# A two-layer diffusion step: the conditioning product moved out of the start and run in column groups, and attention scores issued in pairs

## The reference

```python
def _adaln(cvec, w, b):                      # w: (1024, 6144) for each layer
    m = (jax.nn.silu(cvec) @ w + b).reshape(-1, 1, 6 * D_MODEL)
    return jnp.split(m, 6, axis=-1)
for i in range(DEPTH):                       # DEPTH = 2
    mp = _adaln(c_ctx, mod_w[i], mod_b[i])   # context tokens
    ms = _adaln(c, mod_w[i], mod_b[i])       # latent tokens
    hp = _modulate(_rmsnorm(xp, norm1_g[i]), mp[0], mp[1])   # h * (1 + scale) + shift
    # layer 0: windowed attention (8 heads) and retention on h @ w_in, concatenated, @ w_out
    # layer 1: neighbourhood attention (16 heads) on h @ w_qkv, @ w_out
    xp = xp + mp[2] * op                     # gate
    hp = _modulate(_rmsnorm(xp, norm2_g[i]), mp[3], mp[4])
    # layer 0: dense SwiGLU; layer 1: top-2-of-8 expert SwiGLU
    xp = xp + mp[5] * fp
```

## Time and profile before

| | us |
|---|---|
| median of 3 runs | 2034.63 (2031.91 to 2095.38) |
| the profiled execution | 2029.53 |
| its span, first to last instruction | 2027.9 |
| PE busy in the span | 1842.5 (91%) |
| DVE busy | 1291.8 (64%) |
| ACT busy | 1088.9 (54%) |
| mean granted clock of TensorE | 0.915 |

### The profile page before, as it was taken

How to read it: one execution, slowest core, us unless ns; L and a number is a source line. 1 busy time by engine, 2 the same in 40 slices (tenths; PEclk the granted TensorE clock), 3 DMA queues, 4 the chain that set the end, 5 groups by cost and what they waited for, 6 DMA issues and landing times.

```text
span 2027.9 us, 27794 instructions
## 1 busy us (share of the span) xinstructions
PE 1842.5 (91%) x9817; PEld 1453.8 (72%) x9818; DVE 1291.8 (64%) x1599; ACT 1088.9 (54%) x1493; POOL 154.4 (8%) x225
## 2 busy tenths in 40 slices
PE   4868889999999999999869989999999999999992
PEld 2546677677888877867657868877877777778781
DVE  3764565554434344356537647679898989898985
ACT  3755552433333233356316546567777777777771
POOL 3010010000000004043020000000000000000001
PEclk7879995588999998999859989999999999999996
DMA  8956650022444435422315766789999999999971
GB/s 273 331 174 223 226 184 11 0 86 83 124 124 125 125 107 143 125 68 49 115 53 202 256 245 219 253 314 337 337 337 327 338 325 334 340 334 325 339 267 37
DMA packets 199740, 416.61 MB, mean 205 GB/s; under 512 B 17436, under 2 KB 36948, under 8 KB 199632
## 3 DMA queue, kind: packets, MB, share of 16 engines
q1 hardware_dynamic: 188928, 394.31, 56.8%
q0 software_dynamic: 10704, 20.86, 3.7%
HBM read 415.00 MB, written 5.90 MB: 208 GB/s over the span
## 4 chain that ended last, share of the span: by engine, by line
PE 76%; DVE 11%; ACT 5%; issue 3%; DMA 3%; POOL 0%; SPq 0%; ACTq 0%; DVEq 0%; POOLq 0%
PE ps L522 20%; PE ps L526 19%; PE ps L525 19%; PE ps L954 3%; DVE wlo L495 3%; DMA rawb<-in_mod_w 2%; PE ps L1235 2%; ACT whi L467 2%; PE ps L986 2%; DVE wlo L472 2%; PE ps L964 2%; ACT whi L491 2%; PE ps L1183 1%; PE ps L1254 1%; DVE h L1778 1%
## 5 line engine op out<-in xcount | busy, mean ns | idle before, releaser
L472 DVE TENSOR_TENSOR wlo<-rawb,whi 128x1024 fp32r<-128x1024 f32 x224 | 271.9, 1234 | 344.1 <-ACT whi L467 342.9
L467 ACT ACTIVATE whi<-rawb 128x1024 fp32r<-128x1024 f32 x224 | 231.8, 1055 | 352.2 <-PE ps L526 319.3
L495 DVE TENSOR_TENSOR wlo<-rawb,whi 128x1024 fp32r<-128x1024 f32 x288 | 349.0, 1223 | 111.2 <-ACT whi L491 107.9
L491 ACT ACTIVATE whi<-rawb 128x1024 fp32r<-128x1024 f32 x288 | 304.6, 1060 | 141.1 <-PE ps L526 140.4
L495 DVE TENSOR_TENSOR wlo<-rawx,whi 128x1024 fp32r<-128x1024 f32 x240 | 291.1, 1223 | 56.7 <-ACT whi L491 53.1
L491 ACT ACTIVATE whi<-rawx 128x1024 fp32r<-128x1024 f32 x240 | 254.7, 1061 | 112.8 <-PE ps L526 111.9
L522 PE MATMUL ps<-whi,eT_hi 128*128 128x512 f32 (+1 forms) x768 | 301.7, 393 | 3.8 <-DVE wlo L495 1.9
L525 PE MATMUL ps<-wlo,eT_hi 128*128 128x512 f32 (+1 forms) x768 | 291.1, 379 | 0.0
L526 PE MATMUL ps<-whi,eT_lo 128*128 128x512 f32 (+1 forms) x768 | 291.1, 379 | 0.0
L522 PE MATMUL ps<-whi,hT_hi 128*128 128x512 f32 (+1 forms) x672 | 261.1, 388 | 20.9 <-DVE wlo L472 17.1
L525 PE MATMUL ps<-wlo,hT_hi 128*128 128x512 f32 (+1 forms) x672 | 256.8, 382 | 0.0
(11 more groups left out here) (311 smaller groups left out, 2430.9 us busy)
## 6 DMA issues: line engine op xcount, KB each, us to landing
rawb<-in_od_moe_w_gu SPq DMA_DIRECT2D x192, 512.0 KB, 5.4
rawx<-in_od_moe_w_gu SPq DMA_DIRECT2D x160, 512.0 KB, 5.3
rawb<-in_mod_w SPq DMA_DIRECT2D x96, 512.0 KB, 5.2
rawb<-in_od_moe_w_down SPq DMA_DIRECT2D x96, 512.0 KB, 5.1
rawx<-in_od_moe_w_down SPq DMA_DIRECT2D x80, 512.0 KB, 5.4
rawb<-in_ev_ffn_w_gu SPq DMA_DIRECT2D x44, 512.0 KB, 3.7
rawb<-in_od_w_qkv SPq DMA_DIRECT2D x24, 512.0 KB, 3.6
rawb<-in_ev_w_in SPq DMA_DIRECT2D x22, 512.0 KB, 3.8
```

What stands on the lines that cost most here:

```text
L467: nc.scalar.activation(whi[:, r, :], rawb[:, s, :], ACT.Copy).then_inc(hi_done, 1)
L472: nc.vector.tensor_tensor(wlo[:, r, :], rawb[:, s, :], whi[:, r, :].bitcast(F32), ALU.subtract).then_inc(lo_done, 1)
L491: nc.scalar.activation(whi[:, moe_slot(i), :], moe_raw(j), ACT.Copy).then_inc(hi_done, 1)
L495: nc.vector.tensor_tensor(wlo[:, moe_slot(i), :], moe_raw(i % EB), whi[:, moe_slot(i), :].bitcast(F32), ALU.subtract).then_inc(lo_done, 1)
```

## The change

1. **The form of the conditioning product.** A block is now one k-row x 1024 columns (one whole vector's row), used as float32 straight from the ring: `mod_mm(j)` issues four float32 matmuls of 256 columns, the stationary operand 32 columns wide (`csz`, two of them carry the vectors), each into its own 32 partitions of one PSUM bank. ACT and DVE convert nothing for it; `mod_used` frees the slot. There are still 96 blocks of 512 KB.
2. **Where its blocks stand.** `SEQ` lists all blocks in order. 16 blocks (vectors 0 and 1 of layer 0) stand at the start, 32 behind the first 16 blocks of the input projection, two behind each (`MOD_AFTER`), 8 in `retention()`, one behind each head, and 40 in `attention(0)`, two in each of 20 turns of its loop (`MOD_IN_ATT`). ACT copies a finished vector (`mod_take`), POOL stores it, rows are read back before each norm.
3. **Norm 0** has its statistics before the conditioning product is done (`norm_stats(0)`, `norm_scales(0)`), and makes no gate. The gate of layer 0's mixer is made in the output projection, behind its first two blocks (`gate_first`); its rows lie in `mrow[64:71]`, and `sel_r` grows from 512 to 768 columns.
4. **Banks.** The conditioning product takes bank 4 in retention and attention 0. So `prep` of attention 0 puts keys and queries both into bank 5: it waits for `gn_c` first, and between the two for ACT's copy of the keys.
5. **Attention 1**: PE issues `scores(n)` and `scores(n+1)` of a pair of heads back to back for even n, and nothing at odd n.

The diff, cut to its core:

```diff
+SEQ = [("m", _j) for _j in range(2 * KD)] + [("w", _b) for _b in range(HL)]
+for _b in range(IN_BLOCKS - HL):
+    SEQ += [("w", _b + HL)] + [("m", _j) for _j in MOD_AFTER.get(_b, ())]
+SEQ += [("m", _j) for _j in range(6 * KD, 7 * KD)] + [("w", B_OUT0 + _b) for _b in range(HL)]
+SEQ += [("m", _j) for _j in range(7 * KD, MODS * KD)] + [("w", _b) for _b in range(B_OUT0 + HL, B_MOE)]
+MOD_IN_ATT = {n: (7 * KD + 2 * i, 7 * KD + 2 * i + 1) for i, n in
+              enumerate(n for s in range(2, 23, 5) for n in range(s, s + 4))}
...
+            for p, (kind, i) in enumerate(SEQ):
+                if p >= RAW:
+                    was, n = SEQ[p - RAW]
+                    sp.wait_ge(*((mod_used, n + 1) if was == "m" else (lo_done, n + 1 + RAW)))
...
+            def mod_mm(j):
+                q, k = divmod(j, KD)
+                if k == 0 and q == 6:
+                    pe.wait_ge(up_ev, 1)
+                elif k == 0 and q > 3:
+                    pe.wait_ge(mod_ev, q if q > 6 else q - 1)
+                pe.wait_ge(*landed("m", j))
+                for g in range(4):
+                    mm = nc.tensor.matmul(ps[32 * g:32 * (g + 1), mod_bank(q), 0:2 * P], csz[:, k, :],
+                                          rawb[:, slot_at("m", j), g * 2 * P:(g + 1) * 2 * P], start=(k == 0),
+                                          stop=(k == KD - 1))
+                mm.then_inc(mod_used, 1)
...
+            def gate_first(b):
+                kind = b - B_OUT0
+                if kind not in (0, 1):
+                    return
+                if kind:
+                    pe.wait_ge(gate_ev, 1)
+                else:
+                    pe.wait_ge(mr_l, 2)
+                for half in range(2):
+                    mm = rows_bc(6 + half, 64, 4 + kind, half, 7)
+                mm.then_inc(gate_ps, 1)
...
-                kb, qb = (6, 7) if lay and i == 0 else (4, 5)
+                kb, qb = (6, 7) if lay and i == 0 else (4, 5) if lay else (5, 5)
+                if not lay:
+                    if i:
+                        pe.wait_ge(at_qT, i)
+                    else:
+                        pe.wait_ge(gn_c, 1)
...
+                    if lay == 0:
+                        pe.wait_ge(at_kT, ki + 1)
...
-                    if n < N:
+                    if n < N and (lay == 0 or n % 2 == 0):
                         scores(n)
+                        if lay:
+                            scores(n + 1)
...
+                    if lay == 0:
+                        for j in MOD_IN_ATT.get(n, ()):
+                            mod_mm(j)
...
             def retention():
...
+                    if j < KD:
+                        mod_mm(6 * KD + j)
```

More of the change, by code:

```diff
@@ L82 @@
 _at = 0
-for _name, _n in (("ident", P), ("ones", P), ("before", P), ("slots", CAP), ("experts", E), ("orow", E), ("tok", T), ("sel", 4 * P),
+for _name, _n in (("ident", P), ("ones", P), ("before", P), ("slots", CAP), ("experts", E), ("orow", E), ("tok", T), ("sel", 6 * P),
                   ("ropec", 2 * DH), ("ropes", 2 * DH), ("mask0", 2 * 3 * P), ("ahead", P), ("behind", P),
@@ L729, in _, with mod_store @@
-            pool.wait_ge(mod_out, 16 * (MOD_CH // MOD_STEP))
+                for q in range(3 if n else 2):
+                    c0 = (3 * half + q) * D
+                    pool.dma_start(mrow[32 * q + 4:32 * q + 5, :], mod_b[lay:lay + 1, c0:c0 + D]).then_inc(m_in, 16)
+                if n == 1:
+                    pool.dma_start(mrow[70:71, :], mod_b[0:1, 2 * D:3 * D]).then_inc(m_in, 16)
+            def mod_store(q):
+                pool.wait_ge(mod_ev, q + 1)
+                if q:
+                    pool.wait_ge(mod_out, 16 * q)
+                pool.dma_start(mods[q], mst[:, q % 2, :]).then_inc(mod_out, 16)
@@ new lines, in norm_mods @@
+            def norm_mods(n):
+                first_q = 3 * n
+                pool.wait_ge(mod_out, 16 * (first_q + (3 if n else 2)))
+                for row, q in [(32 * i, first_q + i) for i in range(3 if n else 2)] + [(66, 2)] * (n == 1):
+                    pool.dma_start(mrow[row:row + 2, :].rearrange("p (j n) -> p j n", j=4),
+                                   mods[q].rearrange("(j r) n -> r j n", j=4)[0:2]).then_inc(m_in, 16)
+            norm_rows(0)
+            for q in range(2):
+                mod_store(q)
@@ L1336, in _ @@
             pe.wait_ge(tin_lo, 12)
-            dense(OUT_CH[0], None)
+            dense(OUT_CH[0], None, after=gate_first)
             norm(1, 2)
@@ L1340, in _ @@
             norm(2, 3)
-            dense(QKV_CH, GM_DONE[1], 3, lambda: prep(1, 0))
+            dense(QKV_CH, GM_DONE[1], 4, lambda: prep(1, 0))
             pe.wait_ge(gm_ev, GM_DONE[1] + T * len(QKV_CH) - 4)
@@ L1455, in dense @@
                         if b != ch[-1][0][-1] or proj is None:
-                            ahead.to(min(b + 1 + HL, B_MOE))
-                        for m in mod_behind(b):
-                            mod1(m)
+                            ahead.to(min(b + 1 + HL, limit))
+                        if b in MOD_DONE:
+                            mod_take(MOD_DONE[b])
+                        if after is not None:
+                            after(b)
                     if extra is not None:
@@ L1535, in attention @@
                         prep(lay, n // 6 + 1)
+                    if lay == 0 and n in MOD_IN_ATT and n % 5 == 0:
+                        mod_take(MOD_IN_ATT[n][1] // KD)
             def retention():
@@ L1702, in _ @@
             split_rows(1)
-            dense(OUT_CH[0], None, None)
+            dense(OUT_CH[0], None, None, after=gate_first)
             norm(1, 2)
@@ L1797, in norm, with dense @@
                 turn_in(turn)
-            def dense(ch, extra=None, n=None, hold=False):
+            def dense(ch, extra=None, n=None, hold=False, limit=B_MOE):
                 for c, (bs, o, w) in enumerate(ch):
-                    last = min((N_MOD1[mod_behind(bs[-1])[-1]] if mod_behind(bs[-1]) else bs[-1]) + 1 + HL, B_MOE)
+                    last = min(bs[-1] + 1 + HL, limit)
                     if n is not None:
@@ L2229, in _ @@
             split_rows(0)
+            ahead.to(HL)
             norm(0, 0)
-            dense(IN_CH, tables, hold=True)
+            dense(IN_CH, tables, limit=B_OUT0)
             retention()
```

324 lines of the change are left out of this document (124 added, 200 removed).

## The result

The changed kernel takes 1943.75 us (median of four executions, 1939.29 to 1956.32). Its ratio to the kernel before is 0.9565, with a 95% interval of 0.9521 to 0.9608. The profiled execution took 1939.8 us where the profiled one of before took 2029.5: -89.7 against a forecast of -104.6. So the kernel is faster by about what the prediction said, but one stage inside it went the wrong way.

A forecast was written before the change was run, and what follows sets the result against it. Bounds: DMA weight reads at the start, ACT's conversion chain in the projection, PE in retention and the attentions. Terms -65.2 - 41.4 - 3 + 9 + 1 - 5 = -104.6 take the median from 2034.6 to 1930 us; range 1908 to 1970.

The forecast's parts named there:

- Start: Up to the input projection: 16 blocks in place of 56, projection starting at 75.4 instead of 140.6 us, -65.2.
- Input projection: Input projection: 16 steps of 5.20 us and six of 4.13, in all 113.0 us, -41.4.
- Retention: Retention up to attention 0: eight visits added, clock expected to stay up, longer wait in `prep`; sum -3 us.
- The visits' price of 5.0 at 1.0: In retention: eight visits of one block, 0.63 us each at a clock of 1.0, 5.0 us.
- The other term, 2 for `prep`: `prep` of attention 0 waits for `gn_c`, then for a copy between keys and queries: 2 us.
- The upper bound, +11: Worst case for retention: clock down at once, visits costing 8 x 1.25 us, and no -10.
- Attention 0: Attention 0: twenty visits of two blocks added, clock rising at about unit 8; 78.6 + 3 - 72.5 = +9 us.
- Behind it: After attention 0: gate in the output projection +2, smaller waits +0.5 each, `turn_in(1)` -2; in all +1 us.
- The small rest: All stages outside those priced by the prediction: no change, 0 us.
- Attention 1: Attention 1: paired scores save PE time but DVE becomes the limit, three pairs in 9.5 us; -5 us.
- The rival with the clock at 0.5 through attention 0: Attention 0 never gets the higher clock and costs +42 us, not +9; kernel 1963 us, chance 0.22.

The follow-up runs named there:

- the first experiment: The changed kernel with retention's eight visits of one conditioning block moved behind four more blocks of the input projection; median 1938.2 us.

## Why the prediction was right and wrong

1. *Start*, right: -64.6 for -65.2. Two errors nearly cancelled, which is luck: the store took 5.23 us where I had 3.8 (from a row of 8 KB stores, while the new one has 128 KB), the read with its issue 2.69 where I had 4.5.
2. *Input projection*, right: a visit of two took 1.00 us, a step 5.35. A fourth more blocks, in the first experiment, cost only PE's time, so the DMAs were no bound.
3. *Retention*, **the step that failed**: "the added streams make PE busier, and I expect the clock to stay up there: about half of the PE-bound part, -10". The clock fell 13.4 us in and 42.1 us ran at 0.5. The visits' price of 5.0 at 1.0 was sound, but they cost 12.0 with what they pushed into the low part (first experiment). The other term, 2 for `prep`, was right: without visits the stretch is 2.0 longer than before. The upper bound, +11, was passed by 3: its own terms, 8 x 1.25 and 2, make 12, and it had no room for retention's own work that the visits pushed into the part at 0.5. Of the 12.0, 7.3 are the visits' busy time, and about 4 are, as an estimate, own work that now ran at half the clock (15.5 us of it ran at 1.0 without visits, and 13.4 less three visits of 0.57 with them). The idea itself was right at double the dose, but not dependably: with 16 blocks the clock held in four traces with two a visit and in one with one a visit, and fell after 20.6 us in two others; with 24 it held in the one trace. Why it fell 13.4 us in with eight visits of one and 27.7 with four of two stays open.
4. *Attention 0*, right in kind, too dear: +7.5 with `turn_in`, -0.7 measured. The rise came 16 us in, not 25 to 45, with a second dip of 6.8 us from 276.2 on, and a visit of two took 1.86 us at 0.5 (276.31 to 278.17) where I had 2.1. In the two traced executions with a rise at 58 to 59 us the same code takes 94, between my sum and the rival that never sees it. The change's own executions spread by about as much, 17 us, but no trace ties the two together: the longest of them, 1956.3, has a mean granted clock of 0.923, above the traced one's 0.917. DMA bound it where I said: 0.99 busy at 372 GB/s behind the rise.
5. *Behind it*, right: +2.7. The small rest, +3.9, I had at zero; 1.6 of it lie behind attention 1, where the clock is at 0.95.
6. *Attention 1*, right by size (-4.9 for -5), wrong in its parts, and so partly luck: three pairs take 8.8, not 9.5, which makes -10, since DVE did not become the limit, and a dip of the clock at the start (10.3 us at 0.5), which only the paired form has, gives about 5 back. The larger effect, that unpaired scores may lose the clock altogether, was in no rival of mine: I took the clock of 1.0 there for a property of the stage. It was one of one execution.

The rival with the clock at 0.5 through attention 0 did not come. The traced execution lies 15 us above its forecast (1939.8 for 1925): retention's 17, less attention 0's 8, plus 1.7 for the start and the projection and 4 for the small rest. The median lies 14 above (1943.8 for 1930).

The Trainium skill (TensorEngine Tiling, Key Properties) has a change of tiling mode drain the array. The trace agrees that there is a toll: a visit of one block took 0.57 us at a clock of 1.0 and a visit of two 1.00, so the second block costs 0.43 and the toll is 0.14, where I had 0.18. That the toll is such a drain and nothing else, no run shows.

## What to carry to other kernels

Where narrow matmuls bound a stage, price it at both clocks and ask what decides between them; a clock read in one execution is not the stage's. Work that must be done anyway is worth most where it also keeps PE at its high clock, and then a larger portion can cost less than a small one, so size the portion by several executions and not by its busy time. And when an edit seems worth a few microseconds, look at how the executions spread: the pairs moved the median of the shorter executions by nothing measurable and took a whole group of longer ones away.

## What was unexpected of the hardware

- The same instructions in attention 1 took 89.5 us at a clock of 1.0 and 155.4 with the clock at 0.5 for 150 us without a return, while PE was busy 99% of them. Which of the two properties of a pair holds the clock, that its two scores run at once or that they stand together, was not tried.
- Identical retention code (two blocks a head) lost the clock after 20.6 us in two traces and held it for some 40 in three others. What differs between such executions stays open; retention began at 193.2 to 197.1 us in all of them.
- The DRAM round trip at the start: 5.23 us for the 128 KB store and 2.10 for the read back.
